# Up projection of a two-layer MLP block: plain weight quadrants cast by ScalarE, one token sum made by GpSimd, block 3's casts ahead of a gating function

## What is computed

```
h = rms_norm(x, norm_mlp_pre[l])
u = h @ w_up                                  # [1024 tokens, 1024] x [1024, 5632]
up = jnp.pad(u, ((0, 0), (CONV_WIDTH - 1, 0), (0, 0)))
uc = conv_b + sum(conv_w[j] * up[:, j:j + S] for j in range(CONV_WIDTH))
gate, val = jnp.split(uc, 2, axis=-1)
return (jax.nn.gelu(gate, approximate=True) * val) @ w_down
```

## Time and profile before

| what | value |
|---|---|
| median of 3 runs | 3885.54 us (3884.36 to 3887.36) |
| the profiled execution's own time | 3882.93 us |
| its span, first to last instruction | 3881.1 us |
| mean granted TensorE clock of the span | 0.981 |
| PE busy | 3684.5 us, 95% of the span |
| DVE busy | 2350.3 us, 61% |
| POOL busy | 1975.2 us, 51% |
| ACT busy | 1599.9 us, 41% |
| up projection in blocks of seven products | about 2071 to 2472 us (layer 0) and 3248 to 3648 us (layer 1) |

### The profile page before, as it was taken

One profiled execution on the slowest core, in us unless ns is written; L12 is line 12 of the kernel. 1 busy time (PEld: TensorE's weight loads), 2 busy tenths in 40 slices (PEclk: granted clock), 3 DMA queues, 4 the chain that ended last, 5 costly groups with the idle time before them and its releaser, 6 DMA issues.

```text
span 3881.1 us, 49826 instructions
## 1 busy us (share of the span) xinstructions
PE 3684.5 (95%) x18751; PEld 3036.9 (78%) x18751; DVE 2350.3 (61%) x3614; ACT 1599.9 (41%) x3190; POOL 1975.2 (51%) x1627
## 2 busy tenths in 40 slices
PE   6999999999999998999898999998999898999998
PEld 5888887888888877777686878886878586788886
DVE  4424344836777766544648777776444647777775
ACT  3224231326666653225534333444225533333444
POOL 3223223825555527221536778886222525778884
PEclk9999999999999999999999999999999899999999
DMA  5322222323333103100132222554110132222554
GB/s 183 96 84 91 83 58 94 108 85 102 118 112 119 65 33 106 60 24 15 33 126 76 95 95 82 195 183 148 42 40 21 33 116 81 95 95 82 179 192 142
DMA packets 276298, 367.54 MB, mean 95 GB/s; under 512 B 41605, under 2 KB 159765, under 8 KB 276058
## 3 DMA queue, kind: packets, MB, share of 16 engines
q1 hardware_dynamic: 243448, 289.55, 23.3%
q10 hardware_dynamic: 32610, 74.80, 5.5%
HBM read 281.80 MB, written 80.36 MB: 93 GB/s over the span
## 4 chain that ended last, share of the span: by engine, by line
PE 71%; DVE 17%; ACT 4%; issue 4%; POOL 1%; DMA 1%; SPq 0%; ACTq 0%; DVEq 0%; POOLq 0%
PE ps L130 67%; PE ps L133 4%; DVE ml_p L142 3%; DVE cst_sm L153 3%; ACT thi L136 2%; DVE tfl L142 1%; DVE f_ta L150 1%; DVE f_tb L150 1%; DVE tlo L142 1%; DVE f_tb L142 1%; DMA tfi<-in_ada_w 1%; DVE g_z L142 1%; DVE f_ub L142 1%; ACT ml_o L136 1%; ACT tfi L136 0%
## 5 line engine op out<-in xcount | busy, mean ns | idle before, releaser
L142 POOL TENSOR_TENSOR wlo<-wst,whi 128x512 fp32r<-128x512 f32 (+1 forms) x648 | 969.3, 1505 | 127.8 <-ACT whi L136 96.9
L139 POOL CAST whi<-wst 128x512 fp32r<-128x512 f32 (+2 forms) x368 | 305.9, 831 | 1209.8 <-DMA wst<-in_a_w_in 347.1
L130 PE MATMUL ps<-whi,thi 128*128 128x512 f32 (+3 forms) x2144 | 841.1, 392 | 49.1 <-DVE tlo L142 19.3
L130 PE MATMUL ps<-whi,tlo 128*128 128x512 f32 (+3 forms) x2144 | 815.3, 380 | 0.0
L130 PE MATMUL ps<-wlo,thi 128*128 128x512 f32 (+3 forms) x2144 | 814.3, 380 | 0.0
L130 PEld LDWEIGHTS ps<-whi,thi 128*128 128x128 f32 x2144 | 408.2, 190 | 126.9 <-DVE tlo L142 19.5
L130 PEld LDWEIGHTS ps<-wlo,thi 128*128 128x128 f32 x2144 | 408.4, 190 | 70.8 <-issue 3.8
L130 PEld LDWEIGHTS ps<-whi,tlo 128*128 128x128 f32 x2144 | 406.7, 190 | 71.2
L130 PE MATMUL ps<-thi,whi 128*128 128x512 f32 x856 | 339.9, 397 | 26.4 <-DVE tlo L142 15.3
L130 PE MATMUL ps<-thi,wlo 128*128 128x512 f32 x856 | 335.4, 392 | 0.0
L130 PE MATMUL ps<-tlo,whi 128*128 128x512 f32 x856 | 335.0, 391 | 0.0
(11 more groups left out here) (406 smaller groups left out, 7644.6 us busy)
## 6 DMA issues: line engine op xcount, KB each, us to landing
wst<-in_w_down SPq DMA_DIRECT2D x154, 256.0 KB, 3.5
wst<-in_w_up SPq DMA_DIRECT2D x126, 256.0 KB, 2.9
scr_h<-f_tb SPq DMA_DIRECT2D x44, 512.0 KB, 4.0
wst<-scr_t SPq DMA_DIRECT2D x88, 256.0 KB, 3.1
wst<-in_w_in SPq DMA_DIRECT2D x80, 256.0 KB, 2.7
tfl<-scr_h SPq DMA_DIRECT2D x68, 256.0 KB, 2.8
da_am<-in_ada_w SPq DMA_DIRECT2D x64, 256.0 KB, 2.7
wst<-in_a_w_in SPq DMA_DIRECT2D x72, 192.0 KB, 2.4
```

The source lines that it names most:

```text
L130: return self.none if self.e is None else self.e.matmul(*a, **k)
L139: return self.none if self.e is None else self.e.tensor_copy(*a)
L142: return self.none if self.e is None else self.e.tensor_tensor(*a)
```

## The change

On the up projection alone, three things change. (1) POOL no longer casts A11, A12 and A22; ScalarE casts all seven weight tiles of a block in the order of `PRODUCTS`, after the last sum as before, and POOL is left with seven subtracts. (2) T3 = B22 - B12 is made by POOL as soon as VectorE has made B22, in place of VectorE; ScalarE's cast of T3 waits for it and for T1. VectorE makes the weight sums of block 2 before T4 in place of after it. (3) In the pass for block 2, ScalarE casts block 3's weights right after the copies of block 1 and ahead of `gelu(1)`, in place of behind it. No DMA is added, removed or moved.

```diff
 pool_mlp
+        q.wait_ge(*S.at("t_raw", (l, "B22")))
+        q.tensor_tensor(self.tw["T3"][:], self.tx["T2"][:], self.tx["T3"][:], ALU.subtract).then_inc(*S.up("t_early", (l, "T3")))
         for m in range(2, self.FF):
             slots = self.up_slots(l, m)
             for role, _, _ in self.PRODUCTS:
                 key, s = ("u7", l, m, role), slots[role]
                 if role[0] == "A":
-                    q.wait_ge(*S.at(f"w{s}", key))
                     q.wait_ge(*S.at("u_sum", (l, m, "S4")))
-                    self.split_slot(q, s, key)
-                else:
-                    q.wait_ge(*S.at("s_hi", key))
-                    self.split_slot(q, s, key, hi=False)
+                q.wait_ge(*S.at("s_hi", key))
+                self.split_slot(q, s, key, hi=False)
 act_mlp
         for name in ("T3", "T2", "T1", "T4"):
-            q.wait_ge(*S.at("t_raw", (l, name)))
+            if name == "T3":
+                q.wait_ge(*S.at("t_early", (l, "T3")))
+            q.wait_ge(*S.at("t_raw", (l, "T1" if name == "T3" else name)))
             q.activation(self.th[name][:], self.tw[name][:], ACT.Copy).then_inc(*S.up("t_hi", (l, name)))
...
                 first(1, 0)
                 first(1, 1)
+                self.act_sums_hi(q, l, 3)
             self.act_gelu(q, l, m - 1)
             if m + 1 < self.FF:
-                self.act_sums_hi(q, l, m + 1)
+                if m > 2:
+                    self.act_sums_hi(q, l, m + 1)
 act_sums_hi
-        for role in ("S2", "S3", "S1", "S4"):
+        for role, _, _ in self.PRODUCTS:
             h, _, raw = self.wslot(slots[role])
+            if role[0] == "A":
+                q.wait_ge(*S.at(f"w{slots[role]}", ("u7", l, m, role)))
             q.activation(h, raw, ACT.Copy).then_inc(*S.up("s_hi", ("u7", l, m, role)))
 dve_mlp
         raw("T1", self.tw["T1"][:], b12, self.tw["T1"][:], ALU.subtract)
-        raw("T3", self.tw["T3"][:], b22, b12, ALU.subtract)
         raw("T2", self.tw["T2"][:], b22, self.tw["T1"][:], ALU.subtract)
+        self.dve_up_sums(q, l, 2)
         raw("T4", self.tw["T4"][:], self.tw["T4"][:], self.tw["T2"][:], ALU.subtract)
-        self.dve_up_sums(q, l, 2)
```

## The result

The changed kernel takes 3887.9 us (median of 20 runs, 3881.69 to 3892.86), the kernel before 3883.47 us on the same chip (20 runs): ratio 1.0014, 95% interval 1.0008 to 1.002, that is 3.1 to 7.8 us slower. The forecast was 3886.4 us, 3876 to 3895, most likely no change that 0.2% can tell. The time came within that, but as a loss of 0.14% that 20 runs tell from none: the 0.2% was too coarse. (The median before is 2.1 us lower here than the one shown, so the difference is 4.4 us where +0.9 was forecast.) Not every step under it held.

A forecast was written before the change was run, and what follows sets the result against it. The prediction took VectorE's list, from its low parts to c22 of block 3, to bound the start. Layer 0 at 0, layer 1 at -0.7 and settled blocks at +1.6 gave +0.9 on 3885.54: 3886.4 us, range 3876 to 3895.

The forecast's parts named there:

- The bound of the start: Start of each layer: VectorE's own list, from its low parts to c22 of block 3, sets PE's 6.2 and 6.8 us waits.
- part 4: Way to c22 of block 3: fewer GpSimd casts taking turns with VectorE; gains 1.8 us in layer 0, 0.9 in layer 1.
- Part 1: Start, T3 on GpSimd: it holds VectorE's T2 for the whole instruction; +1.8 us in layer 0, +0.2 in layer 1.
- Part 2: Weight sums ahead of T4: PE's block 2 starts some 1.3 us later, costing nothing under PE's wait ahead of S4.
- Part 3: Block 3's casts ahead of the gating function: PE comes sooner to S4 and waits longer there; 0.
- Rival (c): Start comes out better: split waits keep PE's clock at 2.4 GHz, 2.3 us a layer; no T2 hold, 1.8; 3880.0 us; chance 0.10.
- Part 5, settled blocks: Settled blocks: tap +0.3, convolution steps +0.25, difference tile -0.5; taken as +0.1 us a block, +1.6 on 16 waiting blocks.
- Part 5, later blocks: Later blocks: PE has no idle time and VectorE's list is shorter; 0, at worst +0.3 us on 16 blocks.
- rival (b): Settled and later blocks: ScalarE becomes the link, its late tap costing 0.3 us in 32 blocks, 9.6 us; 3894.4 us; chance 0.13.
- its two signs: Signs of ScalarE as link: waits also after block 13, and the convolution held by f_ta for more than 0.3 us.
- Rival (a): Settled blocks: fewer GpSimd turns free VectorE, c22 comes 0.5 us sooner, small waits close, 8.3 us; 3876.5 us; chance 0.12.

The follow-up runs named there:

- e1: The kernel before with ScalarE casting all seven weight tiles; T3, the order of the sums and block 3's place as before; ratio 1.0006.
- e10: The changed kernel with ScalarE's casts of A12, S4 and A22 behind the tap and VectorE's c22 right behind u3; ratio 0.9957.
- e7: The changed kernel with T3 back on VectorE, ScalarE's casts of A12, S4 and A22 behind the tap, and c22 right behind u3; ratio 0.9962.
- e8: The changed kernel with T3 and the sums' order as before; ratio 1.001.
- e2: The kernel before with T3 on GpSimd and the weight sums of block 2 ahead of T4; ratio 1.0008.
- e4: The changed kernel with one more ScalarE copy, 0.52 us into an unused tile, ahead of the copy of f_ua in blocks 4 to 19; ratio 1.0033.
- e9: The changed kernel with VectorE's c22 right behind u3; ratio 1.001.

## Why the prediction was right, and where it wasn't

**The bound of the start and part 4: right.** S4 of block 3 waits for `f_ub`, 2120.30 us less the 3.13 us by which the stage starts later: 2117.17, against 2117.12. In layer 1 it comes 0.6 us earlier (68.6 against 69.2 us after B12); the forecast had 0 and -0.7 from parts 1 and 4 together. The parts hold one by one too: from the low part of T2 to `c22` of block 3 VectorE takes 49.2 us in both layers, where it took 50.87 and 49.99, -1.7 and -0.8 (forecast -1.8 and -0.9), and e1, which moves the casts alone, shows the same 49.2.

**Part 1: right.** T2 ended at 2065.31 - 3.13 = 2062.18 us; forecast 2062.2. T3 ended at 2063.16 and T2 2.15 us behind it, where T2's whole length alone is 2.29: GpSimd's instruction held VectorE for its whole length, as the Trainium skill (SBUF — State Buffer, section "SBUF: two separate sides") has it. Its price of +1.8 us in layer 0 and +0.2 in layer 1 is what e10 shows against e7 (1.73 and 0.20). Against e8 it is nothing, because there ScalarE's cast of T2 is late by itself: `f_T2l` starts 18.39 us after B12 in e8, 18.51 in the changed kernel, 16.79 before. The sum's 1.8 us hang on that cast being in time, and that changes from run to run: the cast starts 14.8 us after B12 in six of the thirteen profiled runs in layer 0, the kernel before among them, and 16.4 us in the others, the changed kernel among them. So whether T3 has a price is chance in each run.

**Part 2: right, with its cover.** PE starts block 2 1.3 us later in layer 0 (24.20 against 22.89 us after B12; forecast 1.3) and 0.6 in layer 1. It cost nothing, as S4 of block 3 starts where it did or sooner. What the order of the sums is worth by itself isn't shown: e2 has it together with T3 on GpSimd.

**Part 3: worth nothing, as said, but not by the wait named.** The forecast had PE come sooner to S4 and wait longer there. It first waits 3.3 us at A12 for `m1`. That copy stands on ScalarE behind the two taps of block 2, and they wait for VectorE's `c12` of block 2 and for the store behind its `gate` of block 1 (changed kernel, ScalarE):

```profile
2108.60 1.24 ACT L136 ACTIVATE f_ta<-f_ua,tfi 128x1024 f32<-128x1024 f32 x1 [7.51 <-DVE f_ua L142]
2111.12 1.24 ACT L136 ACTIVATE f_tb<-f_ub,tfi 128x1024 f32<-128x1024 f32 x1 [1.27 <-DMA scr_h<-f_tb]
2112.27 0.58 ACT L136 ACTIVATE tfi<-ps 128x512 f32<-128x512 f32 x1
```

Beside e1, PE starts block 3 3.7 us sooner (46.7 against 50.4 us after B12, layer 0) and so runs into an earlier link of the same list of VectorE's; the forecast looked behind the casts only as far as `gelu(1)` and the gate. The copy ends 61.1 us after B12, 59.1 before. The 9.6 us of block 3's two waits before (3.4 + 6.23) became 8.8 (2.6 + 3.33 + 2.83).

**Rival (c) isn't shown.** In layer 0 S4 starts where it did, yet block 3 ends 0.9 us sooner (75.85 against 76.77 us after B12). PE now works between the waits, and the 5 us behind the last are granted 0.66 with 15 matmuls, against 0.50, the 1.2 GHz level, with 12. But in layer 1 block 3 ends 0.5 us sooner only because S4 starts 0.6 us sooner: from S4 to the block's end it is 7.24 us before, behind one wait of 6.75 us, and 7.34 after, behind three shorter ones. In the layers of the thirteen runs these 24 matmuls take 5.7 to 8.6 us, and in e1 5.7 and 7.3 behind the same waits. So the 0.9 us of layer 0 can't be put down to the waits being split. Window of the changed kernel, layer 0, columns as in the earlier trace rows:

```profile
2120.30:2125.30 5.00, 5.00 (x15) 3.96 (x16) 1.43 (x3) 3.91 (x8) 3.14 (x3) 0.66 0.01 3
```

**Part 5, settled blocks: terms right, one undersized.** The convolution came 0.27 us later behind its turn (forecast 0.3), the difference gave 0.5 us back (forecast 0.5), but the four steps took 8.07 us, 0.39 more than before, where the step "0.2 + 4 x 1.08 + 3 x 1.15 = 7.9: +0.25" had less. 0.27 + 0.39 - 0.5 = +0.16 us a block; +0.1 was taken. Over blocks 4 to 12 the loss is 1.4 and 0.7 us a layer.

**Part 5, later blocks: the step that failed.** "In the later blocks PE has no idle time and VectorE's list is shorter by the difference: 0". A PE that is always busy says that nothing can be gained there, not that nothing can be lost. They lose 1.1 us a layer (block 12 to block 21: 172.0 before, 173.1 after). PE's waits list nothing there, but the timelines of VectorE and ScalarE show it, here over two late blocks of the changed kernel:

```profile
2421.36 3.61 DVE L150 SCALAR_TENSOR_TENSOR f_ta<-f_ua,tfi,f_ta 128x1024 f32<-128x1024 f32 x2 [0.20 <-ACT f_ta L136]
...
2433.69 1.28 DVE L142 TENSOR_TENSOR wst<-wst 128x512 f32<-128x512 f32 x2
...
2440.56 3.59 DVE L150 SCALAR_TENSOR_TENSOR f_ta<-f_ua,tfi,f_ta 128x1024 f32<-128x1024 f32 x2 [0.18 <-ACT f_ta L136]
...
2435.01 3.76 ACT L136 ACTIVATE whi<-wst 128x512 fp32r<-128x512 f32 x7 [8.94 <-DVE wst L142]
```

The convolution waits for the tap as in a settled block, and comes every 19.20 us, more than PE's 19.04. That is loop 2, which the forecast never closed: it priced the tap's 0.3 us as a delay within one block and took what VectorE won later as free. In a loop the next casts start from the last sum, so the tap's delay returns. From the timelines: before, loop 1 took 2255.35 - 2235.72 = 19.63 us (`c22` to `c22`), and loop 2 would have taken 4.02 (last sum's end 2237.60 to tap's end 2241.62) + 14.32 (convolution 2242.92 to last sum's end 2257.24) = 18.34; three casts and the longer convolution, less the difference, bring loop 2 to 5.59 + 14.21 = 19.80 (2240.74 to 2246.33 to 2260.53), and it sets the block. Loop 1 came down to 7.20 + 12.32 = 19.52 (`c22` 2238.86, turn of the convolution 2246.06; convolution 2246.33, next `c22` 2258.65). Without the difference tile's 0.6 us it is 19.20 in the later blocks. So rival (b) was the mechanism, at 0.17 and 0.12 us a block in place of 0.3; of its two signs, the convolution is held by `f_ta` for 0.2 us, not more than 0.3, and no wait of PE's is listed after block 13. Rival (a), closed waits, did not come: the convolution's four steps grew from 7.68 to 8.07 us.

**The sum.** Forecast: start -0.7, settled +1.6, later 0, together +0.9. Measured in the stage: start -1.5, blocks 4 to 12 +2.2, later +2.2, together +2.9 us. That the sum is only 2 us off is in part luck: 0.9 us of the start's 1.5 is layer 0's, where S4 starts no sooner, and it hides part of the later blocks' loss. The +2.9 is a little under the lower end, 3.1 us, of the timed difference; the rest isn't explained. The stretches outside the stage vary by up to 5 us between profiled runs (from block 21 of layer 0 to B12 of layer 1: 746.9 to 751.8 us) with no link to the edits that I can see.

## What to carry to other kernels

Two engines that feed each other once per block form loops, and a block takes the longest loop. Before work is moved to an "idle" engine, add up each loop through it; an instruction added to a loop costs time once the loop's slack (here 1.3 us) is used up, also where nobody is seen to wait: of 0.52 us in e4, 0.3 us a block. Where an edit to one loop gives nothing, look for a second loop of nearly the same length before dropping it: in the changed kernel the split casts and the early `c22` were worth nothing alone and 0.4% together. And try the edit where the loop is alone: in the kernel before, the early `c22` brought that 0.4% by itself.

## What the runs showed of the hardware

A VectorE sum of 128x512 that reads what the instruction just before it wrote, and waits for it at a semaphore, starts 0.79 us behind that one's start, where others follow at 0.60 (e9: `c22` at 2252.72 behind `u3` at 2251.93, against 2250.80 behind 2250.20). That makes loop 2 of e9 0.2 us longer than the changed kernel's.

Whether ScalarE's cast of T2 is in time hangs on a granted clock that differs between the two layers of one run. The kernel before, the 6 us from B12 on, layers 0 and 1 (columns as in the earlier trace rows):

```profile
2048.63:2054.63 6.00, 5.89 (x26) 4.89 (x27) 5.93 (x3) 1.24 (x3) 0.00 (x0) 1.00 0.30 97
3224.26:3230.26 6.00, 5.88 (x19) 4.71 (x20) 5.93 (x3) 1.24 (x3) 0.00 (x0) 0.72 0.15 58
```

A clock of 1.00 is the 2.4 GHz level; the 0.72 is a mean of stretches at 0.50, the 1.2 GHz level, and at 1.00. With it PE gets through 19 matmuls in place of 26; block 0's copies on ScalarE, and the cast of T2 behind them, come 1.6 us later (16.42 against 14.82 us after B12). In the 12 us ahead PE was busy for 10.19 us in both layers. What decides between the two isn't shown.
